# Hybrid encoder block on eight cores: groups 0 and 1 pass as a pair behind shared weight slabs

## What is computed

```
h = rms_norm(x); lru_x, lru_gate, q, k, v = split(h @ w_in)        # 1024 -> 2560
lru_x = causal_dwconv(lru_x, width 4); r, i = sigmoid(block_diag(lru_x))
a = exp(-8 r softplus(-lam)); h_t = a h_{t-1} + sqrt(1 - a^2) i x  # scan over positions
out_a = gelu(lru_gate) * h
out_b = (softmax(q1 k1) - lam softmax(q2 k2)) v, rms_norm          # 4 heads, chunk-causal, T5 bias
x = x + concat(out_a, out_b) @ w_out                               # 1024 -> 1024
gate, val = split(rms_norm(x) @ w_up)                              # 1024 -> 2 * 3072
x = x + (gelu(causal_dwconv(gate, width 3)) * val) @ w_down        # 3072 -> 1024
out = rms_norm(x)
```

## Time and profile before

| | |
|---|---|
| median of 3 runs | 1809.09 us (lowest 1808.4) |
| profiled execution | 1817.51 us, span of its slowest core 1816.0 us |
| spans of the eight cores | 1797.6 to 1816.0 us |
| busy of 1816.0 us | PE 1752.8, PEld 818.0, DVE 1171.2, ACT 1100.6, POOL 437.1 |
| moved | 372.04 MB by all transfers of the core, 205 GB/s |

### The profile page before, as it was taken

How to read it: one execution, slowest core, us unless ns; L and a number is a source line. 1 busy time by engine, 2 the same in 40 slices (tenths; PEclk the granted TensorE clock), 3 DMA queues, 4 the chain that set the end, 5 groups by cost and what they waited for, 6 DMA issues and landing times.

```text
span 1816.0 us, 32704 instructions; the slowest of 8 cores (1797.6 to 1816.0 us)
## 1 busy us (share of the span) xinstructions
PE 1752.8 (97%) x9779; PEld 818.0 (45%) x9779; DVE 1171.2 (64%) x2041; ACT 1100.6 (61%) x1450; POOL 437.1 (24%) x619
## 2 busy tenths in 40 slices
PE   8999989999999999999899999999999999999997
PEld 3444444444444444444344444444444444444443
DVE  3778875369573576647784496727676376756834
ACT  5768795468862686636754366626865478842711
POOL 1435651025430121202421141202212031201300
PEclk9999999999999999999999999999999999999999
DMA  9995799987897543738568745685447644347533
GB/s 286 287 309 172 229 304 273 312 278 240 263 281 206 187 156 106 235 121 254 168 193 227 242 167 162 191 230 174 162 136 213 210 162 144 95 144 205 192 139 139
DMA packets 177133, 372.04 MB, mean 205 GB/s; under 512 B 74560, under 2 KB 74816, under 8 KB 176832
## 3 DMA queue, kind: packets, MB, share of 16 engines
q1 hardware_dynamic: 176960, 369.95, 64.8%
HBM read 294.40 MB, written 59.77 MB: 195 GB/s over the span
## 4 chain that ended last, share of the span: by engine, by line
PE 75%; ACT 6%; issue 6%; DMA 5%; DVE 5%; POOL 1%; SPq 1%; DVEq 0%; ACTq 0%; POOLq 0%
PE pb L857 38%; PE pb L875 26%; PE pb L1082 6%; PE pb L1049 4%; ACT PT L1071 2%; DMA KT<-w_up 1%; DMA Va<-w_up 1%; ACT aT L1177 1%; DMA Va<-w_in 1%; DMA xr<-x 1%; ACT raw L934 1%; DMA KT<-w_in 1%; PE pb L707 1%; DVE xf L1218 1%; DVE aT L1185 1%
## 5 line engine op out<-in xcount | busy, mean ns | idle before, releaser
L857 PE MATMUL pb<-hT,ringF 128*128 128x512 bf16 x3072 | 710.9, 383 | 14.0 <-DVE aT L1185 5.5
L857 PEld LDWEIGHTS pb<-hT,ringF 128*128 128x128 bf16 x3072 | 287.4, 98 | 373.3 <-issue 75.9
L1071 ACT ACTIVATE PT<-pb,prm 128x1024 bf16<-128x1024 f32 (+1 forms) x288 | 306.0, 1062 | 153.5 <-PE pb L1049 72.8
L875 PE MATMUL pb<-ringF,aT 128*128 128x512 bf16 x1536 | 357.9, 381 | 0.1
L1200 DVE TENSOR_TENSOR xf<-pb,xf 128x512 f32<-128x512 f32 x192 | 132.2, 690 | 211.0 <-PE pb L875 210.4
L843 POOL TENSOR_TENSOR sm<-sm 128x1 f32<-128x1 f32 (+1 forms) x128 | 102.4, 805 | 671.0 <-DVE sm L840 664.3
L857 PE MATMUL pb<-hT,ringA 128*128 128x512 bf16 x1024 | 244.0, 383 | 8.9 <-DVE raw L934 2.7
L875 PEld LDWEIGHTS pb<-ringF,aT 128*128 128x128 bf16 x1536 | 146.4, 98 | 178.2 <-issue 15.6
L1185 DVE TENSOR_TENSOR aT<-pb,aT 128x512 bf16<-128x512 f32 x192 | 131.0, 687 | 115.5 <-PE pb L857 114.9
L1082 PE MATMUL pb<-Va,PT 128*128 128x129 bf16 x2176 | 171.1, 221 | 7.5 <-ACT PT L1071 4.8
L1082 PEld LDWEIGHTS pb<-Va,PT 128*128 128x128 bf16 x2176 | 140.7, 98 | 79.4 <-issue 37.0
(11 more groups left out here) (131 smaller groups left out, 1728.4 us busy)
## 6 DMA issues: line engine op xcount, KB each, us to landing
ringF<-wslab SPq DMA_DIRECT2D x240, 512.0 KB, 4.4
ringA<-wslab SPq DMA_DIRECT2D x98, 512.0 KB, 5.6
xr<-x SPq DMA_DIRECT2D x64, 512.0 KB, 7.4
Va<-w_up SPq DMA_DIRECT2D x37, 512.0 KB, 6.6
wslab<-ringF SPq DMA_DIRECT2D x36, 512.0 KB, 6.7
KT<-w_up SPq DMA_DIRECT2D x35, 512.0 KB, 6.6
x<-xr SPq DMA_DIRECT2D x32, 512.0 KB, 4.5
xf<-x SPq DMA_DIRECT2D x32, 512.0 KB, 7.6
```

The lines of the kernel that those rows point to most:

```text
L857: last = e.matmul(bank(p), lhsT=w[:, kk, cc * 128:(cc + 1) * 128], rhs=src[:, hf * 4 + kk, :], start=(hf == 0 and kk == 0), stop=(hf == 1 ...
L875: last = e.matmul(bank(p), lhsT=src[:, k0 + hf * 4 + kk, t * 128:(t + 1) * 128], rhs=w[:, kk, :], start=(hf == 0 and kk == 0), stop=(hf == ...
L1071: op("act", act_us(2 * N, ptr=1), lambda e, s=s, pt=pt, N=N, h=h: e.activation(out=PT[:, pt.s, :, 0:N], in_=psum[:, s.s:s.s + 2, 0:N], fun ...
```

## The change

Groups 0 and 1 go through the opening together:

- **Shared slabs.** A (`stage_A(*gis)`), G and C take both groups for each slab. The FFN of both goes by thirds of its width (8 of 24 feature blocks): `stage_P` does gate, GeLU, value and down of one third. The plan is third 0 of group 0, third 1 of group 0, third 0 of group 1, third 1 of group 1, and third 2 of both together. L and B stay separate (each L loads its own slabs).
- **x in SBUF.** The x tiles of the two groups are loaded once and stay until the last norm (`stage_E`); these groups neither read x again for C nor write and read `x1`. The down projections of the thirds add into them.
- **Places.** `place(1)` puts group 1's `hT`, `mixT` and `hT2` into the three thirds of `aT`, and its q into a slot. Group 0's gate work on the first third of `aT` comes after group 1's last use of its `hT` (`more`).
- **One pool.** `ringA`, `ringF`, `xr` and `xf` become `slot`, 21 slots of 4 KB a partition, with classes F (4), A (6), XF (4) and X (7); a slot holds an x tile, a bf16 slab or a float32 staging piece. `NPT` goes from 4 to 3.
- **No second cast.** `late` is gone: each slab is cast and written back at its first use. Only third 2 stages through the later buffers and slots.
- **Order.** New fractions for the stages of groups 0 and 1, for those of groups 2 to 7 (`FR`), and for the shift of each group's L, B, C, N and A (`e_`).

The core of the diff; the renaming of buffers, G, C and the moving of code into helpers are left out:

```diff
-    NRA, NRF, NPT, NXR = 6, 4, 4, 6
+    NPT, NSL = 3, 21
...
+        q1 = VT(P_S, cls="X")
+
+        def place(gi):
+
+            if gi == 1:
+                return (aT[:, 0:8, :], b_hT1, lambda: slotb[:, q1.s, :].rearrange("p (h q) -> p h q", h=4), [q1] * 4,
+                        aT[:, 8:16, :], b_aT[8:16], aT[:, 16:24, :], b_hT21)
+            return hT, b_hT, lambda: qT, b_qT, mixT, b_mix, hT2, b_hT2
...
+        NP = 2
+        x0 = [[load_x(x_d, gi, t, ("XF", "X")[gi], pri=-8 + 2.12 * gi) for t in range(NT)] for gi in range(NP)]
...
-            late = key[0] in ("up",) and key[2] == 1 and ngrp > 2
-            if uses[key] <= (2 if late else 1):
...
+            if uses[key] == 1:
                 st_, sn = P_st, 1
-                b_st = b_stg if uses[key] == 1 and key[0] != "dn" else b_stg1
+                third = key[1] % 6 // 2 if key[0] == "up" else key[1] % 3 if key[0] == "dn" else 0
+                b_st = b_stg if third < LOTH else b_stg1
...
+        def stage_A(*gis):
...
+            sl = [load_slab(("in", 2, hf), "A", pr) for hf in range(2)]
+            for gi in gis:
+                S_.grp = gi
+                hT, b_hT, qT_, b_qT_ = place(gi)[:4]
+                for h in range(4):
+                    p = mm_fm(sl, h, hT, b_hT, after=([b_qT_[h]] if gi != 1 else []) + stg)
+                    evac(p, (lambda h=h: qT_()[:, h, :]) if gi == 1 else qT[:, h, :], b_qT_[h], scale=0.125, stg=stg)
...
+        def gate_units(gi, sl, f0, at):
+
+            hT2, b_hT2 = place(gi)[6:]
             fw = pv("fcw").rearrange("p (c k) -> p c k", c=24)
-            if first:
-                op("pool", 0.6, lambda e: e.memset(fhalo[:], 0.0), writes=b_fhalo)
-            cur = None
-            units, convs = [], []
-            for fc in range(24):
-                if fc % 4 == 0:
-                    cur = [load_slab(("up", fc // 4, hf), P_F, ringF, pr) for hf in range(2)]
-                p = mm_fm(cur, fc % 4, hT2, b_hT2, after=[b_aT[fc]])
-                units.append(p.pe)
+            us, cs = [], []
+            for i in range(4):
+                fc, a = f0 + i, at + i
+
+                more = b_hT1 if gi == 0 and fc < 8 and a < 8 else b_hT21 if gi == NP and a >= 16 else []
+                p = mm_fm(sl, i, hT2, b_hT2, after=[b_aT[a]], behind=last_gate)
+                last_gate[:] = [p.pe]
+                us.append(p.pe)
                 r_ = conv_in(p, 2, fhalo[:, fc, :], b_fhalo[fc])
                 a_ = VT(P_fa)
-                n = conv(r_, 2, facc, a_, fw[:, fc, :], pv("fcb", fc, fc + 1), aT[:, fc, :], b_aT[fc])
-                convs.append(n)
+                cs.append(conv(r_, 2, facc, a_, fw[:, fc, :], pv("fcb", fc, fc + 1), aT[:, a, :], [b_aT[a]] + more))
+            return us, cs
...
+        def stage_P(third, at, line="F"):
+
+            pr = S_.pri
+            units, convs = [], [[], []]
+            gis = sorted(at)
+            last_gate[:] = []
+            for s_ in range(2):
+                sl = up(2 * third + s_, pr, line)
+                for gi in gis:
+                    u, c = gate_units(gi, sl, third * 8 + s_ * 4, at[gi] + s_ * 4)
+                    units += u
+                    convs[gi] += c
+            for gi in gis:
+                for s_ in range(2):
+                    gelu(at[gi] + s_ * 4, [convs[gis[0]][7]], "p%d%d" % (third, gis[0]))
+            for s_ in range(2):
+                sl = up(6 + 2 * third + s_, pr, line)
+                for gi in gis:
+                    value_units(gi, sl, at[gi] + s_ * 4)
+            for c2 in range(2):
+                sl = dn(c2, third, pr, line)
+                for gi in gis:
+                    down_units(sl, c2, at[gi], x0[gi])
+            return units
...
+        FR.update({'N': (-0.5, -0.372), 'A': (-0.163, 0.141), 'F1': (0.226, 0.275), 'G': (0.246, 0.304), 'F2': (0.382, 0.621), 'F3': (0.733, 1.021), 'L': (0.426, 0.714), 'B': (-0.06, 0.547), 'C': (0.645, 0.806)})
+        both = list(range(NP))
...
+        PR.update({'N0': (-6.483, -6.38), 'N1': (-6.091, -6.088), 'A': (-5.838, -5.301), 'G0': (-6.221, -6.266), 'L0': (-5.302, -4.564), 'L1': (-4.817, -3.395), 'B0': (-5.395, -4.633), 'B1': (-4.505, -3.624), 'C': (-4.474, -2.824)})
+        paced(0, *PR["N0"], stage_N, 0)
+        paced(0, *PR["N1"], stage_N, 1)
+        i0 = len(S_.nodes)
+        paced(0, *PR["A"], stage_A, *both)
...
+        paced(0, *PR["L0"], stage_L, 0)
+        paced(0, *PR["L1"], stage_L, 1)
+        bq = paced(0, *PR["B0"], stage_B, 0)
+        paced(0, *PR["B1"], stage_B, 1)
+        paced(0, *PR["C"], stage_C, both)
+        paced(-5, 0, 0, stage_H)
+        units = None
+        plan = [(0, {0: 0}, 'F', -4.706, -3.414), (1, {0: 0}, 'F', -3.522, -2.449), (0, {1: 8}, 'A', -0.324, 0.794), (1, {1: 0}, 'A', 0.153, 1.267), (2, {0: 8, 1: 0}, 'F', 1.084, 2.146)]
+        for third, at, line, f0, f1 in plan:
+            u1 = units
+            units = paced(0, f0, f1, stage_P, third, at, line)
+        for gi in both:
+            paced(0, 2, 2, stage_E, gi)
+        e_ = {2: -0.097, 3: -0.022, 4: 0.046, 5: -0.047, 6: 0.016, 7: 0.182}
...
+                    return {"F": range(0, 4), "A": range(4, 10), "XF": range(10, 14), "X": range(14, 21), "hi": (9, 8, 20, 19)}[v.cls]
```

More of the change, by code:

```diff
@@ L122, in node @@
         n.stg = ""
+        n.grp = self.grp
         n.soft = set()
@@ L722, in build @@
         stg_ap = {P_st: [kst(2), vst(8), kst(3), vst(12)],
[L723 to L726, removed]
+                  P_S: [slot[:, i, :] for i in range(NSL)]}
+        dn_stage = itertools.cycle([(P_st, 1), (P_S, 1)])
         def w_src(key):
@@ L785, in load_slab @@
                     casts.setdefault(line, []).append(n)
-                if uses[key] == (2 if late else 1):
-                    node({"sp": 0.1}, lambda e: e.dma_start(out=wsl_d[si], in_=ring[:, v.s, :]), reads=[v],
-                         writes=[b_slabd[si]], dma=524288, pri=pri, tag="wb")
+                node({"sp": 0.1}, lambda e: e.dma_start(out=wsl_d[si], in_=ring[:, v.s, :]), reads=[v],
+                     writes=[b_slabd[si]], dma=524288, pri=pri, tag="wb")
             else:
@@ L953, in conv @@
                     in1=tile[:, v.s, :], op0=ALU.mult, op1=ALU.add), reads=[r_, b_prm] + ([v] if last else []),
-                   writes=[b_out] if last else [v], tag="conv")
+                   writes=b_out if last else [v], tag="conv")
             return nd
@@ L958, in build, with stage_L, lru @@
         HALO = {"pool": 0.35, "dve": 0.13}
-        def stage_L(gi):
+        def stage_L(*gis):
+            pr = S_.pri
+            sl = [load_slab(("in", 0, hf), "F" if gis[0] == 0 else "A", pr) for hf in range(2)]
+            for gi in gis:
+                lru(gi, sl)
+        def lru(gi, sl):
             seq, g = groups[gi]
+            hT, b_hT, _, _, mixT, b_mix = place(gi)[:6]
             first = (g == 0)
@@ L1131, in stage_B, with stage_C @@
             return [first_qk]
[L1133 to L1134 removed]
+        def stage_C(gis, behind=()):
             pr = S_.pri
[L1136 to L1139 removed]
+            sl = [[load_slab(("out", c2, hf), "A", pr) for hf in range(2)] for c2 in range(2)]
+            for gi, t in itertools.product(gis, range(NT)):
+                mixT, b_mix, hT2, b_hT2 = place(gi)[4:]
+                xi = gi % 2
+                v = x0[gi][t] if gi < NP else load_x(x_d, gi, t, "X", behind=behind)
                 for c2 in range(2):
@@ new lines, in value_units, with down_units, add @@
+        def value_units(gi, sl, at):
+            hT2, b_hT2 = place(gi)[6:]
+            for i in range(4):
+                a = at + i
+                p = mm_fm(sl, i, hT2, b_hT2, after=[b_aT[a]])
+                op("dve", dve_us(512), lambda e, p=p, a=a: e.tensor_tensor(out=aT[:, a, :], in0=bank(p), in1=aT[:, a, :],
+                                                                           op=ALU.mult),
+                   reads=[p], writes=[b_aT[a]], tag="val")
+        def down_units(sl, c2, at, vx):
+            for t in range(NT):
+                p = mm_tm(sl, t, aT, b_aT[at:at + 8], k0=at, tag="dn", soft=[vx[t].ld])
+                def add(e, c2=c2, v=vx[t], p=p):
+                    xs = slot[:, v.s, c2 * 512:(c2 + 1) * 512]
+                    return e.tensor_tensor(out=xs, in0=bank(p), in1=xs, op=ALU.add)
+                op("dve", dve_us(512), add, reads=[p], writes=[vx[t]], tag="res")
@@ L1172, in stage_F1 @@
+        def stage_F1(gi):
+            pr = S_.pri
+            if groups[gi][1] == 0:
+                stage_H()
+            units, convs = [], []
+            for k in range(6):
+                u, c = gate_units(gi, up(k, pr), 4 * k, 4 * k)
+                units += u
+                convs += c
             return units, convs
```

223 lines of the change are left out of this document (113 added, 110 removed).

## The result

The median fell from 1809.09 us (3 runs) to 1792.94 us (1792.24 to 1794.82, 4 runs), a ratio of 0.991 [0.989, 0.993]. The forecast was 1763: a gain of 16 us where 46 were foreseen. In some executions the cores of one die, at times of both, show a lower granted clock and take some per cent longer; medians and ratios in this document leave these executions out, and for e1 to e8, where one die was disturbed in nearly all of them, spans of cores of the other die are compared. The profiled execution of the changed kernel has a span of 1791.2 us on core 0, its slowest.

The account below looks back on a forecast made before the run. Ahead of 600 us waits for float32 weights bound the kernel, afterwards TensorE. Of 104.3 us lost there, 22 + 24 + 12 would remain, a gain of 46: 1809.1 - 46 = 1763 us (chance 0.58), range 1720 to 1815.

Parts of the forecast that it names:

- What bounds the kernel: Whole kernel: TensorE loses 146.2 us, 104.3 ahead of 600 us to waits for float32 weights; after that TensorE is the bound.
- Transfers: Groups 0 and 1: 60 issues fewer, 31.5 MB, 120 us of DMA time at 262 GB/s in the first 600 us.
- The start: 0 to 50 us: loss falls from 36.3 to 22 us, as the 14.4 us of filler after 25 us go.
- 50 to 300 us: That stretch of the opening: loss falls from 56.3 to 24 us, keeping 21.7 idle and 2 of filler.
- The signs of being wrong: Idle growing from 100 to 250 us, first up-projection after 150 us, or loss after the pair changing by over 11 us.
- 300 to 600: That stretch in us: the loss of 11.7 us stays as 12, bounds 6 and 20.
- Groups 2 to 7: After the pair: only priorities move; effect taken as 0, with 11 us either way.
- Casts and thirds: FFN of groups 0 and 1: 48 casts fewer and five passes instead of two, both taken as 0.
- the 17 us for three more turns: FFN of the pair: three added passes, each with a 5.5 us turn, cost 17 us if nothing fills them.
- ACT and DVE are the wall; no change: Rival for the opening: only the start improves, loss to 600 us 107, time 1808 us; chance 0.20.
- The LRU chain: Rival: group 0's FFN waits for group 1's LRU projections, starting near 212 us; loss 134, time 1839 us; chance 0.08.
- The third: Rival: all foreseen waits vanish, no loss from 50 to 300 us; 87 us gained, time 1722 us; chance 0.14.

Follow-up runs that it names:

- e1: The changed kernel with the old fractions and shifts for the stages of groups 2 to 7: core 0 1803.8 to 1809.7 us.
- e8: The changed kernel without the attention's bias additions and per-head norm in groups 0 and 1: mean span of cores 4 to 7 1774.8 us.
- e9: The kernel before with 60 stores of 512 KB added over the work of groups 0 and 1: 1865.8 us, ratio 1.029.
- e16: The changed kernel with 60 stores of 512 KB added over the pair's work, moving the kernel before's bytes: 1830.6 us, ratio 1.012.
- e10: The changed kernel itself, unaltered, measured again beside other runs: 1794.4 us, ratio 0.990 to the kernel before.
- e14: The kernel before without the attention's bias additions and per-head norm in groups 0 and 1: 1817.4 us, ratio 1.002.
- e15: The changed kernel without the attention's bias additions and per-head norm in groups 0 and 1: 1784.6 us, ratio 0.982 to the kernel before.
- e13: The changed kernel with altered places in aT and other opening fractions (group 0's LRU earlier, group 1's LRU and projections later): 1780.1 us, ratio 0.980.
- e11: The kernel before, no pair, with the change's new fractions and shifts from group 2's FFN on: 1796.5 us, ratio 0.991.
- e3: The kernel before without `late`, each half slab of w_up cast once: core 0 1805.9 to 1821.8 us.
- e12: The changed kernel with the old fractions and shifts for groups 2 to 7: 1807.5 us, ratio 0.997 to the kernel before.
- e6: The changed kernel with group 1's `hT2` in aT's first third, group 0's FFN writing the last: cores 4 to 7 1794.7, 1785.4, 1793.0, 1783.8 us.

## Why the prediction was wrong

- *What bounds the kernel.* That the loss lies mostly ahead of 600 us was right; "from 600 us TensorE is the bound" passed over 41.9 us of loss, of which 15.7 went. That "the opening waits for the float32 weights" is half of it: in the kernel before the transfers share the opening with the other engines (e9). In the changed one they don't hold 100 to 200 us, where the queue stands for 44.
- *Transfers.* 31.5 MB less, as counted: 340.54 MB. They were worth something, 24 us of loss and some 36 us of time by e16 against e10. What the sum lacked is the price of the order that saves them, which is as large.
- *The start.* 22 forecast, 23.0 measured, of that 18.9 filler ahead of the first slab. Right.
- *50 to 300 us: the step that failed.* "I keep the 21.7 idle and 2 of filler: 24" came out at 64.1 (25.3 idle, 38.8 filler). I weighed bytes against TensorE time over the stretch as a whole (229 against 232 to 256 us) and gave filler to the transfers ("foreseen waits (filler) should mostly go"). But a row of filler names no releaser: the planner foresees waits for ACT and DVE as well, and between 100 and 150 us it now puts in 21.9 us where DVE is busy 44.9 of 50. It did so before the change too, as the matmul behind a filler would have told (core 2):

```profile
131.56 1.68 PE L707 MATMUL pb<-zero 128*128 128x512 bf16 x7
133.85 0.39 PE L1049 MATMUL pb<-qT,KT 64*128 64x512 bf16 x2 [0.60 <-ACT PT L1071]
```

  In e14, the kernel before with less DVE work, the filler of this stretch falls from 34.3 to 23.7 us (means of eight cores). What I left out is when ACT and DVE work falls due: the pair puts two LRUs and two attentions ahead of the first gate matmul, so TensorE has little but what these two engines hand it. The rows at 129 to 136 us show that wait, and e15 beside e14 and e13 beside e10 what it is worth: less work for DVE, or another order of the mixing, gives 10 and 14 us, and the first of these gives nothing in the kernel before. For ACT alone no run shows its share.
- *The signs of being wrong.* All three came: idle from 100 to 250 us grew from 11.7 to 21.4 us (means of eight cores) with waits for ACT and DVE, the first gate matmul started at 178.8 us, and the loss after the pair changed by 15.7.
- *300 to 600.* 12 forecast, 17.6 measured, within its bounds (6 to 20).
- *Groups 2 to 7, "taken 0".* The second failed step, with the other sign: 41.9 to 26.2 us, 15.7 won where 11 was the bound. e11 shows that this is the fractions' doing and needs no pair.
- *Casts and thirds* at 0 are in line with e3 and with the loss of 17.6 from 300 to 600 us; the 17 us for three more turns can't be told apart there.
- *The rivals.* "ACT and DVE are the wall; no change" had the opening right, almost to the figure (107 foreseen, 104.7 measured), but in part by luck: it has nobody waiting for the saved bytes, and e16 gives them 24 us, which the order's price happens to cancel. Nor are ACT and DVE the only wall: e14 meets the weights next. Its 1808 left out the fractions, as the forecast did; e12, the pair without them, is at 1807.5. "The LRU chain" named the right neighbourhood and the wrong wait: the FFN started at 178.8, but e6 takes the wait for `hT` away and nothing moves. The third, with all foreseen waits gone, is refuted by 38.8 us of filler. (Its "under 290" holds for the stretches of the earlier trace rows; the earlier trace rows has 317 GB/s from 25 to 50 us.)

So the forecast's direction was right for a reason other than mine, and its sum was 46 where the opening gave 0 and the rest 16. The Trainium skill ("Perfetto Trace Analysis", Optimization Strategy) says that where the most-contended engine changes over time, interleaving the regimes may help; the runs agree with it so far as e13, another mix of the same work, has 0.980 against 0.990.

e13 is the fastest kernel of this study: it loses 28.6 us less than the kernel before (147.6 to 119.0), 15.4 of it after 600 us, by the fractions, and 13.2 in the opening. What holds the other 90.8 us there was not taken apart further.

## What to carry to other kernels

Before a stretch is called transfer-bound, ask who released each wait in it, filler included (the matmul behind a filler names it), and lay the work of every engine in the order in which it will fall due: sums over a stretch hide a backlog ahead of a stage. A change that saves a resource and reorders work has two prices; put the saved resource back alone (here 60 idle stores) and the other price is seen. And test a retuning of the rest on the old kernel, or its gain will be read as the change's.

## What the hardware showed unexpectedly

- A gap of TensorE costs more than itself. In e14 (core 1) it was idle from 220 to 225 us, and the granted clock was 0.50 (1.2 of 2.4 GHz) until 245 though it was busy 16.6 of these 20 us. In the changed kernel (core 0) it was busy 1.07 of the 5 us from 195, and the clock was 0.50 from 200 to 205 and 0.93 in the next 5.
- Transfers cost time in a kernel whose queue stands idle part of the time: 24 us of loss for 31.5 MB in the pair (e16), most of it after 250 us, long after the standstill. Part of a price hides in "busy": another 9.5 us of e16 are useful matmuls that ran longer.
